# A four-branch decoder layer: when the projection's input is normalised, and where its gates are applied

## The chip, the cores and the metric

The kernel runs on one core of a Trainium2 chip. The metric is the device time of one execution in microseconds (us), as the median of several runs. The core's engines run side by side, each with a queue of its own that is worked off strictly in order: TensorE (matrix products; PE in the profile, its weight loads PEld), VectorE (DVE), ScalarE (ACT), GpSimd (POOL) and SyncE (SP, which here only issues DMA). An engine that meets a wait on a semaphore stands still with all that is queued behind it. TensorE reads only SBUF and writes PSUM; the PSUM has eight banks of 2 KB per partition.

## The reference, cut to what matters

Two layers of a hybrid decoder run over 256 prompt rows and 8 sample rows (264 columns in the kernel, which keeps features on the partitions). One layer:

```python
x = x + 0.5 * swiglu(rmsnorm(x, norm_ffn1), ...)
h = rmsnorm(x, norm_mix)                      # y = x * rsqrt(mean(x*x) + eps) * g
proj = h @ w_in                               # 3360 RWKV + 1536 short conv + 1544 Mamba columns
p_rwkv, p_sc, p_ssm = split(proj)
# RWKV group: token shift first
xs = p_rwkv + (prev - p_rwkv) * mu            # prev: the row before, or the state
r, k, v, w_lr, a_lr, g_lr = split(xs)         # then decay, keys' norm, LoRA gates, recurrence
# short convolution group
b_gate, c_gate, xt = split(p_sc, 3)
y_sc = rmsnorm(b_gate * causal_conv(c_gate * xt), sc_norm)
# Mamba group: convolution, silu, chunked scan (segments, scores), sample states
x = x + concat(y_rwkv, y_sc, y_ssm) @ w_out
x = x + 0.5 * swiglu(rmsnorm(x, norm_ffn2), ...)
```

## The kernel before, in words

Each layer has a front stage (first FFN, the projection, all that leads up to the recurrence) and a back stage (recurrence, output projection, second FFN). This case is about the second half of the front stage, the projection.

Weights are float32. A product is made in three fp32r products: weight and input are each split into a high part and a low rest. Per tile of 128 output columns TensorE multiplies 8 times (the 8 tiles of the 1024 features) by `hi*x_hi`, `hi*x_lo`, `lo*x_hi` (lines 232 to 234): 24 products of 264 columns. ScalarE makes `hi` of a weight tile (`split_hi`, line 209), VectorE or GpSimd makes `lo` (`split_lo`, line 216; GpSimd has the even tiles 14 to 24, and 44 and 46). Four such pairs are in a ring, so `split_hi(n + 4)` waits until product n is done.

The projection has 51 tiles, n = 0 to 50, each with a kind: n = 0 the tail (last RWKV columns and `dt`), 1 to 8 `xbc`, 9 and 10 RWKV tiles 24 and 25 (LoRA inputs), 11 to 14 `z`, 15 to 18 `x` of the short convolution, 19 to 22 its gate `c`, 23 to 26 its gate `b`, 27 to 34 the RWKV keys (8 to 15), 35 to 42 receptance (0 to 7), 43 to 50 values (16 to 23). The input of the products is `x * gain`, not yet divided by the root mean square; the factor `rs` (a row per column, the same on every partition) is multiplied in when VectorE evicts the tile from PSUM (`evict`, lines 1153 and 1159). Three PSUM banks take turns: product n + 3 waits for the eviction of tile n.

An RWKV tile is evicted to `prev`; ScalarE then writes `xs = (1 - mu) * prev` (line 1122) and keeps the last rows (`last`, line 1124); VectorE adds `mu` times the shifted columns (`shift`, line 1132). For a `c` tile VectorE multiplies a second time, into `u` (line 1162); for `b` all four tiles go to a buffer and one product over all four is made later (line 1290).

All other work of the front stage is woven into this sequence by hand. Every engine has a program `side`, a generator whose `yield s` says "what follows belongs to slot s"; `more.go(n)` in the loop over tiles runs what is due up to slot n. On VectorE, TensorE and GpSimd it stands after the work on tile n, on ScalarE before it. In each engine's queue the order is thus fixed. What matters here, by slot:

- TensorE: 12 transposes of `xa` into `b_tok`'s bank (line 1426), which wait for ScalarE's last SiLU (line 1004); 13, 15, 17, 19 a broadcast of two rows of `cum` (line 1443): the first waits for ScalarE's copy `b_tok` (line 1015), the others for VectorE's segments of the slot before; 16 to 22, even, products with the scores; 26 and 32 broadcasts of B and C rows for the sample states (line 1405), 26 also products with `xdt`; 35 mean of the short convolution's squares; 37 transposes of new states; 38 mean of the SSM squares (line 1507); 39 on LoRA products (line 1520 on), key norms and bonus products (line 1538).
- VectorE: 2 to 9 the Mamba convolution; 10 `cum_lo` and the sample convolution (lines 1212, 790 to 796); 11 `xdt`; 14, 16, 18, 20 segments (lines 1233, 1235, 1237); 15 to 21, odd, scores; 26 and 27 the four short convolutions; 28, 30, 33, 35 sample states (`sample`, `sample_out`); from 36 keys, gates and sums.
- ScalarE: 2 to 11 taps and SiLU; 13 `b_tok`; 15 on exponentials; 25 and 26 decay of the sample states (line 1047, 8 instructions per state tile); 27, 29, 32, 34 `outer` (line 1059), each after the first waiting for `sample_out` of the one before; 40 on the gates (lines 976 to 987), with a batch of Ln and Exp over the norms (lines 1091 to 1097) in slot 45, ahead of `gates(5)`.

## Time and profile before

| | |
|---|---|
| time, median of 3 runs | 1659.33 us (1658.1 to 1665.26) |
| profiled execution, its own time | 1660.52 us |
| its span in the profile | 1658.5 us |
| TensorE busy | 1550.0 us (93% of the span) |
| VectorE busy | 1145.6 us (69%) |
| ScalarE busy | 860.9 us (52%) |
| GpSimd busy | 264.0 us (16%) |
| mean granted TensorE clock | 0.986 |
| projection, layer 0 | 217.4 to 436.2 us |
| projection, layer 1 | 1033.0 to 1251.8 us |

The busy shares are averages over all stages. The time between the first product of the projection and the first of the back stage is what the change can touch. Matmuls are pipelined, so that a TensorE shown as busy can still have short gaps.

### The profile page before, as it was taken

How to read it: one execution, taken by the hardware profiler on the slowest of the kernel's cores; microseconds unless marked ns; L12 is line 12 of the kernel's file. 1: busy time of each engine (PE TensorE's matmuls, PEld its weight loads, DVE VectorE, ACT ScalarE, POOL GpSimd, SP SyncE). 2: the span in 40 equal slices, each digit the busy share in tenths (PEclk: the TensorE clock that was granted, in tenths of full speed). 3: DMA queues.
4: the chain of work that ended last, by engine and by line, in shares of the span. 5: the costliest groups of instructions: out<-in, count | busy, mean ns of one | idle time of the engine just before them, and what ended most of it. 6: DMA issues, size and time to landing. Idle time of an engine off the chain costs nothing. (4 is left out here: it accounts for less than half of the span.)

```text
span 1658.5 us, 41230 instructions
## 1 busy us (share of the span) xinstructions
PE 1550.0 (93%) x17275; PEld 1471.9 (89%) x17275; DVE 1145.6 (69%) x1832; ACT 860.9 (52%) x1521; POOL 264.0 (16%) x259
## 2 busy tenths in 40 slices
PE   7999999989799899999999999998997989899997
PEld 6999999977688789999999999998775878899997
DVE  6565578795798667665575656978768977676654
ACT  5444465767444555444354444657673445554443
POOL 0000003001455531000000000030014554300000
PEclk9999999999899999999999999999998999999999
DMA  7555557471244445555454655654703453465552
GB/s 232 178 168 176 161 157 211 131 210 52 64 127 119 138 150 171 196 174 187 149 186 153 203 166 175 194 157 131 213 1 104 126 166 111 130 199 181 187 176 71
DMA packets 280649, 256.26 MB, mean 155 GB/s; under 512 B 48054, under 2 KB 268700, under 8 KB 280450
## 3 DMA queue, kind: packets, MB, share of 16 engines
q1 hardware_dynamic: 276698, 252.05, 49.3%
q8 instruction: 138, 2.26, 0.6%
q10 hardware_dynamic: 3768, 1.59, 0.4%
q14 instruction: 45, 0.37, 0.1%
HBM read 242.22 MB, written 11.38 MB: 153 GB/s over the span
## 5 line engine op out<-in xcount | busy, mean ns | idle before, releaser
L209 ACT ACTIVATE front_hi<-front_raw 128x1024 fp32r<-128x1024 f32 (+2 forms) x230 | 238.5, 1039 | 257.2 <-PE ps L234 249.7
L216 DVE TENSOR_TENSOR front_lo<-front_raw,front_hi 128x1024 fp32r<-128x1024 f32 (+1 forms) x210 | 252.2, 1201 | 112.5 <-ACT front_hi L209 111.7
L209 ACT ACTIVATE out_hi<-out_raw 128x1024 fp32r<-128x1024 f32 (+1 forms) x168 | 173.2, 1038 | 216.1 <-PE ps L234 202.5
L216 DVE TENSOR_TENSOR out_lo<-out_raw,out_hi 128x1024 fp32r<-128x1024 f32 (+1 forms) x148 | 183.3, 1239 | 109.9 <-ACT out_hi L209 109.3
L232 PE MATMUL ps<-front_h_hi,front_hi 128*128 128x264 f32 (+1 forms) x816 | 241.2, 296 | 8.6 <-DVE front_lo L216 6.7
L234 PE MATMUL ps<-front_h_hi,front_lo 128*128 128x264 f32 (+1 forms) x816 | 233.0, 286 | 0.0
L233 PE MATMUL ps<-front_h_lo,front_hi 128*128 128x264 f32 (+1 forms) x816 | 232.8, 285 | 0.0
L232 PE MATMUL ps<-ffn_h_hi,out_hi 128*128 128x264 f32 x704 | 200.4, 285 | 0.1
L233 PE MATMUL ps<-ffn_h_lo,out_hi 128*128 128x264 f32 x704 | 199.6, 284 | 0.0
L234 PE MATMUL ps<-ffn_h_hi,out_lo 128*128 128x264 f32 x704 | 199.6, 283 | 0.0
L232 PE MATMUL ps<-in_h_hi,front_hi 128*128 128x264 f32 x688 | 197.3, 287 | 0.0
L233 PE MATMUL ps<-in_h_lo,front_hi 128*128 128x264 f32 x688 | 196.4, 285 | 0.0
L234 PE MATMUL ps<-in_h_hi,front_lo 128*128 128x264 f32 x688 | 196.3, 285 | 0.0
L232 PEld LDWEIGHTS ps<-front_h_hi,front_hi 128*128 128x128 f32 (+1 forms) x816 | 154.0, 189 | 16.8 <-issue 14.2
L233 PEld LDWEIGHTS ps<-front_h_lo,front_hi 128*128 128x128 f32 (+1 forms) x816 | 154.2, 189 | 0.7
L234 PEld LDWEIGHTS ps<-front_h_hi,front_lo 128*128 128x128 f32 (+1 forms) x816 | 153.5, 188 | 0.1
L216 POOL TENSOR_TENSOR front_lo<-front_raw,front_hi 128x1024 fp32r<-128x1024 f32 (+1 forms) x20 | 49.8, 2491 | 540.6 <-ACT front_hi L209 540.6
L232 PEld LDWEIGHTS ps<-ffn_h_hi,out_hi 128*128 128x128 f32 x704 | 132.4, 188 | 0.5 <-ACT ffn_h_hi L283 0.5
L233 PEld LDWEIGHTS ps<-ffn_h_lo,out_hi 128*128 128x128 f32 x704 | 132.4, 188 | 0.1
L234 PEld LDWEIGHTS ps<-ffn_h_hi,out_lo 128*128 128x128 f32 x704 | 132.4, 188 | 0.0
L233 PEld LDWEIGHTS ps<-in_h_lo,front_hi 128*128 128x128 f32 x688 | 131.2, 191 | 0.1
L232 PEld LDWEIGHTS ps<-in_h_hi,front_hi 128*128 128x128 f32 x688 | 131.1, 190 | 0.1
(410 smaller groups left out, 3861.2 us busy)
## 6 DMA issues: line engine op xcount, KB each, us to landing
front_raw<-in_w_in SPq DMA_DIRECT2D x50, 1024.0 KB, 5.4
out_raw<-in_ffn_w_in SPq DMA_DIRECT2D x44, 1024.0 KB, 5.2
front_raw<-in_ffn_w_in SPq DMA_DIRECT2D x40, 1024.0 KB, 5.3
back_sample_rows<-row_scratch SPq DMA_DIRECT2D x160, 128.0 KB, 3.1
out_raw<-in_w_out SPq DMA_DIRECT2D x16, 1024.0 KB, 5.8
front_raw<-in_ffn_w_out SPq DMA_DIRECT2D x16, 896.0 KB, 5.0
out_raw<-in_ffn_w_out SPq DMA_DIRECT2D x16, 896.0 KB, 4.9
front_raw<-in_ffn_w_out SPq DMA_DIRECT2D x8, 1024.0 KB, 5.4
```

What stands on the lines that cost most here:

```text
L209: act.activation(self.hi[n % self.RING][:, 0:k, 0:w], self._raw(n), ACT.Copy).then_inc(self.hi_ready, 1)
L216: eng.tensor_tensor(self.lo[n % self.RING][:, 0:k, 0:w], self._raw(n), self.hi[n % self.RING][:, 0:k, 0:w].bitcast(F32), ALU.subtract).the ...
L232: pe.matmul(out, hi[:, j, 0:w], x_hi[:, j], start=start and j == 0, stop=False)
L233: pe.matmul(out, hi[:, j, 0:w], x_lo[:, j], start=False, stop=False)
L234: mm = pe.matmul(out, lo[:, j, 0:w], x_hi[:, j], start=False, stop=stop and j == k - 1)
```

## The change

Tiles 0 to 18 are computed as before, from `x * gain` (now held in `env.in_hi` and `env.in_lo`). Meanwhile VectorE and ScalarE make a second input, `x * gain * rs`, split in `h_hi` and `h_lo`: per feature tile k one step `normed(k)` and one `normed_lo(k)` on VectorE and one `normed_hi(k)` on ScalarE, in slots 10 to 18. From tile 19 on (`NORMED = 19`; the twentieth tile) the products use that, so that what stands in PSUM is final: a `c` tile is multiplied onto `u` straight from PSUM, a `b` tile onto the convolution's result, and an RWKV tile goes without `prev`: ScalarE writes `xs` and `last` from PSUM, then VectorE adds the shifted columns from PSUM (`mix_shifted`) and frees the bank. The `b` tiles move from 23 to 26 to 31 to 34, behind the keys, which are now 23 to 30; two of the four short convolutions move from slots 26 and 27 to 31 and 32, the squares of the short convolution to slot 35 of ScalarE with a buffer of their own, its mean to slot 36 of TensorE. ScalarE's batch of Ln and Exp is cut in two halves, slots 46 and 47, behind `gates(5)`.

```diff
-("c", SC0 + 512, 0, 4), ("b", SC0, 0, 4), ("rwkv", 8 * P, 8, 8), ("rwkv", 0, 0, 8),
+("c", SC0 + 512, 0, 4), ("rwkv", 8 * P, 8, 8), ("b", SC0, 0, 4), ("rwkv", 0, 0, 8),
-        H = len(tiles)
+        H, NORMED = len(tiles), 19
-        z, bg = at("z", 20832, [P, 4, N]), at("b_gate", 25056, [P, 4, N])
+        z, sc_squares = at("z", 20832, [P, 4, N]), at("sc_squares", 25056, [P, 4, N])
-        norm2 = Norm(st, env, "mix", lambda k: env.col("norm_mix", k), A, h_hi, h_lo, rs, xa, ctmp[:, 0])
+        norm2 = Norm(st, env, "mix", lambda k: env.col("norm_mix", k), A, env.in_hi, env.in_lo, rs, xa, ctmp[:, 0])
...
 # GpSimd, slot 42
                     pool.wait_ge(s("state_out"), 64)
+                    pool.wait_ge(s("sc_ms"), 1)
...
 # ScalarE
+                def normed_hi(k):
+                    act.wait_ge(s("normed"), k + 1)
+                    act.activation(h_hi[:, k], ctmp[:, k % 2], ACT.Copy).then_inc(s("normed_hi"), 1)
...
                         yield slot
+                        if slot == 11:
+                            normed_hi(0)
                         if slot < 10:
...
+                    yield 12
+                    normed_hi(1)
                     yield 13
+                    normed_hi(2)
                     act.wait_ge(s("btok_ps"), 1)
                     act.activation(btok[:].rearrange("p c g n -> p (c g n)"), ps[:, A, :], ACT.Copy).then_inc(s("btok_done"), 1)
                     yield 14
+                    normed_hi(3)
...
                         yield 15 + h // 2 * 2
+                        if h in (0, 2):
+                            normed_hi(4 + h)
+                            normed_hi(5 + h)
...
-                        if m == 3:
-                            act.wait_ge(s("sc_gated"), 1)
-                            act.wait_ge(s("bc_ps"), 2)
-                            act.activation(sq, acc, ACT.Square).then_inc(s("sc_sq"), 1)
...
+                    yield 35
+                    act.wait_ge(evicted, 35)
+                    act.activation(sc_squares[:], acc, ACT.Square).then_inc(s("sc_sq"), 1)
                     yield 37
                     act.wait_ge(s("y_gated"), 1)
-                    act.wait_ge(s("sc_ms"), 1)
+                    act.wait_ge(s("bc_ps"), 2)
...
                     for p, slot in enumerate((40, 41, 42, 43, 44, 45, 48, 49)):
-                        yield slot
-                        if p == 5:
+                        if p == 6:
+                            yield 46
                             act.wait_ge(s("norm_max"), RT)
...
+                            yield 47
                             act.wait_ge(s("norm_ln"), 3)
...
+                        yield slot
                         gates(p)
...
 # ScalarE, loop over the tiles
                     more.go(n)
+                    if kind == "rwkv" and n >= NORMED:
+                        act.wait_ge(ws.used, base + n + 1)
+                        bank = ps[:, n % 3, 0:N]
+                        act.activation(mix.xs[:, m], bank, ACT.Copy, scale=env.omu[:, m:m + 1]).then_inc(kept, 1)
+                        act.activation(last[:, m], bank[:, T - 1:T + NS], ACT.Copy).then_inc(last_in, 1)
                     ws.split_hi(act, base + n + 4)
-                    if kind in ("rwkv", "tail"):
+                    if kind in ("rwkv", "tail") and n < NORMED:
...
 # VectorE
+                    if kind == "c":
+                        dve.wait_ge(evicted, n)
+                        dve.tensor_tensor(u[:, m, 2:2 + N], u[:, m, 2:2 + N], bank, ALU.mult).then_inc(evicted, 1)
+                        return
+                    if kind == "b":
+                        dve.wait_ge(s("smp_sc"), 5)
+                        dve.wait_ge(s("uconv"), 3 * (m + 1))
+                        dve.tensor_tensor(acc[:, m], acc[:, m], bank, ALU.mult).then_inc(evicted, 1)
+                        return
...
+                def mix_shifted(n, m):
+                    q, bank = order.index(m), ps[:, n % 3, 0:N]
+                    dve.wait_ge(kept, q + 1)
+                    dve.wait_ge(last_in, q + 1)
+                    dve.scalar_tensor_tensor(out=mix.xs[:, m, 1:T], in0=bank[:, 0:T - 1], scalar=env.col("rwkv_mu", m),
+                                             in1=mix.xs[:, m, 1:T], op0=ALU.mult, op1=ALU.add).then_inc(evicted, 1)
+
+                def normed(k):
+                    if k >= 2:
+                        dve.wait_ge(s("normed_lo"), k - 1)
+                    dve.scalar_tensor_tensor(out=ctmp[:, k % 2], in0=env.x[:, k], scalar=env.col("norm_mix", k), in1=rs[:],
+                                             op0=ALU.mult, op1=ALU.mult).then_inc(s("normed"), 1)
+
+                def normed_lo(k):
+                    dve.wait_ge(s("normed_hi"), k + 1)
+                    dve.tensor_tensor(h_lo[:, k], ctmp[:, k % 2], h_hi[:, k].bitcast(F32), ALU.subtract).then_inc(s("normed_lo"), 1)
...
                     yield 10
+                    normed(0)
                     dve.wait_ge(s("cum_hi"), 1)
...
                     yield 11
+                    normed(1)
                     dve.wait_ge(s("tok_in"), 1)
...
+                    yield 12
+                    normed_lo(0)
+                    normed(2)
+                    yield 13
+                    normed_lo(1)
+                    normed(3)
                     for j in range(4):
                         yield 14 + 2 * j
+                        if j < 2:
+                            for t in (2 + 2 * j, 3 + 2 * j):
+                                normed_lo(t)
+                                normed(t + 2)
+                        if j == 2:
+                            normed_lo(6)
+                            normed_lo(7)
                         for h in (2 * j, 2 * j + 1):
...
 # VectorE, slots 26 to 36: short_conv(0) in 26, (1) in 27, sample(0) 28, conv_sample 29, sample(1) 30,
 # short_conv(2) 31, short_conv(3) and the new states 32, sample(2) 33, sample(3) 35, sc_root and y_gated 36
...
 # VectorE, loop over the tiles
+                    late = kind == "rwkv" and n >= NORMED
-                    if n < H:
+                    if n < H and not late:
                         evict(n, kind, m)
...
                     if n + 3 < H and ws.on_dve[base + n + 3]:
                         ws.split_lo(dve, base + n + 3)
+                    if late:
+                        mix_shifted(n, m)
                     more.go(n)
...
 # TensorE
-                    yield 35
+                    yield 36
                     pe.wait_ge(s("sc_sq"), 1)
...
+                def normed_ready(j):
+                    pe.wait_ge(s("normed_lo"), j + 1)
...
+                    hi, lo = (env.in_hi, env.in_lo) if n < NORMED else (h_hi, h_lo)
+                    ws.product(pe, base + n, ps[0:halves[base + n][2], n % 3, 0:N], hi, lo,
+                               ready={0: norm2.pe_ready(pe), NORMED: normed_ready}.get(n))
```

## Rows read from the trace of the kernel before

**Rows 1.** Stretches: start:end, length, busy of each engine (instructions), granted clock, DMA share, GB/s.
```profile
261.00:303.00 42.00, 41.33 (x332) 37.91 (x332) 30.91 (x72) 22.84 (x32) 13.21 (x5) 1.00 0.53 164
303.00:369.00 66.00, 58.75 (x454) 56.71 (x450) 58.54 (x101) 45.60 (x113) 0.16 (x1) 0.97 0.60 174
...
1033.00:1251.80 218.80, 198.46 (x1469) 179.62 (x1467) 172.14 (x323) 142.19 (x278) 28.20 (x22) 0.98 0.45 133
```

**Rows 2.** TensorE by line, 217.4 to 436.2: busy us, mean ns, idle before and releasers.
```profile
L232 PE MATMUL ps<-front_h_hi,front_hi 128*128 128x264 f32 x400 | 118.3, 296 | 3.7 <-DVE front_lo L216 3.4 <-DVE z L1159 0.2
...
L1520 PE MATMUL ps<-xs,w_a 64*128 64x264 f32 x16 | 5.7, 435 | 1.3 <-ACT conv_new_rows L1078 0.8 <-ACT gate L987 0.5
...
L1538 PE MATMUL ps<-r_k,cst 128*128 128x264 f32 x16 | 5.1, 444 | 4.3 <-DVE r_k L1334 4.3
...
L1405 PE MATMUL ps<-bc_rows,pick_row 16*128 16x256 f32 x16 | 2.3, 284 | 2.5 <-DVE outer L1173 2.5
...
L1507 PE MATMUL ps<-xbc_conv,cst 128*128 128x264 f32 x8 | 2.0, 399 | 1.2 <-ACT xbc_conv L1070 1.2
```

**Rows 3.** A stretch of layer 0 with a low granted clock, columns as in rows 1.
```profile
339.20:342.40 3.20, 3.20 (x17) 3.20 (x16) 3.20 (x11) 3.20 (x11) 0.00 (x0) 0.50 0.12 14
```

**Rows 4.** VectorE by line and shape, 217.4 to 436.2, columns as in rows 2.
```profile
L216 DVE TENSOR_TENSOR front_lo<-front_raw,front_hi 128x1024 fp32r<-128x1024 f32 x40 | 48.6, 1215 | 1.8 <-ACT front_hi L209 1.8
...
L1153 DVE TENSOR_TENSOR front_prev<-ps,front_norm_rs 128x264 f32<-128x264 f32 x26 | 11.1, 428 | 18.4 <-PE ps L234 18.4
...
L1334 DVE SCALAR_TENSOR_TENSOR r_k<-xs,cols 128x264 f32<-128x264 f32 x8 | 3.6, 483 | 0.0
...
L1162 DVE TENSOR_TENSOR gated<-gated,c_gate 128x264 f32<-128x264 f32 x4 | 1.7, 433 | 0.1
```

**Rows 5.** ScalarE in order of time: start us, us, instruction [idle before, releaser].
```profile
260.82 0.49 ACT L1004 ACTIVATE xbc_conv<-xbc_conv,cols 128x256 f32<-128x256 f32 x1
...
263.59 0.58 ACT L1015 ACTIVATE b_tok<-ps 128x512 f32<-128x512 f32 x1
...
308.24 4.78 ACT L1047 ACTIVATE sample_state<-sample_state,spread 128x128 f32<-128x128 f32 x16
...
401.32 1.28 ACT L1091 ACT_TABLE_LOAD   x1
...
409.66 1.28 ACT L976 ACT_TABLE_LOAD   x1
```

**Rows 6.** VectorE in order of time, projection and start of the back stage.
```profile
261.82 0.41 DVE L1212 TENSOR_TENSOR cum_rows<-cum,cum_rows 8x256 fp32r<-8x256 f32 x1
...
263.87 2.35 DVE L796 TENSOR_TENSOR xbc_conv<-xbc_conv,outer 128x64 f32<-128x64 f32 x1
...
266.40 0.42 DVE L1159 TENSOR_TENSOR z<-ps,front_norm_rs 128x264 f32<-128x264 f32 x1
...
273.09 0.14 DVE L1237 COPY cum_last<-ps 128x1 f32<-128x1 f32 x1
...
279.76 0.14 DVE L1237 COPY cum_last<-ps 128x1 f32<-128x1 f32 x1
...
442.96 1.74 DVE L2133 SCALAR_TENSOR_TENSOR bonus<-bonus,cols,gate 128x264 f32<-128x264 f32 x2
```

**Rows 7.** TensorE in order of time: the broadcasts of slots 13, 15 and 17.
```profile
266.17 0.50 PE L1443 MATMUL ps<-cum_rows,pick_row_far 40*128 40x256 f32 x2
...
273.31 0.47 PE L1443 MATMUL ps<-cum_rows,pick_row_far 40*128 40x256 f32 x2
...
280.74 0.50 PE L1443 MATMUL ps<-cum_rows,pick_row_far 40*128 40x256 f32 x2
```

**Rows 8.** GpSimd in order of time: two weight splits, one step of the back stage.
```profile
263.76 2.38 POOL L216 TENSOR_TENSOR front_lo<-front_raw,front_hi 128x1024 fp32r<-128x1024 f32 x1 [4.13 <-ACT front_hi L209]
...
278.11 2.63 POOL L216 TENSOR_TENSOR front_lo<-front_raw,front_hi 128x1024 fp32r<-128x1024 f32 x1 [4.05 <-ACT front_hi L209]
...
443.54 0.87 POOL L1750 TENSOR_TENSOR back_a_r<-kk_normed,back_decays 128x256 f32<-128x256 f32 x1
```

More of the change, by code:

```diff
@@ L1264, in side @@
                                           ALU.mult).then_inc(s("xde_done"), 1)
-                    done = 0
-                    for i in range(4):
-                        yield 26 + i // 2
-                        if i == 0:
-                            dve.wait_ge(s("xa_smp"), 1)
-                            dve.wait_ge(s("spread_in"), 1)
-                            dve.tensor_tensor(xs_dt[:], xa[:, 0:4, T:N], spread[:, :, NS:2 * NS], ALU.mult).then_inc(s("xs_dt"), 1)
-                        dve.wait_ge(s("u_done"), ST)
-                        done = conv_prompt(dve, s("uconv"), acc[:, i, 0:T], u[:, i], lambda j: env.col("sc_conv_w", 4 * j + i), 3, done)
@@ new lines, in side @@
+                    yield 27
+                    short_conv(1)
+                    yield 28
+                    sample(0)
+                    sample_out(0)
+                    yield 29
+                    scb = env.scb[:].rearrange("p m (b j) -> p m b j", j=2)
+                    conv_sample(dve, s("smp_sc"), acc[:, :, T:N], scn[:, :, 0:NS], [scb[:, :, :, 0], scb[:, :, :, 1], u[:, :, 2 + T:2 + N]],
+                                lambda j: env.col("sc_conv_w", 4 * j, 4))
+                    yield 30
@@ new lines, in side @@
+                    sample(1)
+                    sample_out(1)
+                    yield 31
+                    short_conv(2)
+                    yield 32
+                    short_conv(3)
+                    dve.wait_ge(s("smp_sc"), 5)
+                    cvb = env.conv[:].rearrange("p m (b j) -> p m b j", j=3)
+                    scw = scn[:, :, 2:18].rearrange("p m (b j) -> p m b j", j=2)
+                    cvw = cvn[:, :, 3:27].rearrange("p m (b j) -> p m b j", j=3)
+                    dve.tensor_copy(scn[:, :, 0:2], u[:, :, T:T + 2]).then_inc(s("new_in"), 1)
@@ L1301, in side @@
+                    yield 33
+                    sample(2)
+                    sample_out(2)
+                    yield 35
+                    sample(3)
+                    sample_out(3)
+                    yield 36
+                    dve.wait_ge(s("sc_ms"), 1)
+                    dve.tensor_scalar(sc_root[:], ps[:, EB, 0:N], D / SC, NORM_EPS, ALU.mult, ALU.add).then_inc(s("sc_read"), 1)
                     dve.wait_ge(s("smp"), 4)
@@ L1390, in _ @@
                         before = tiles[n - 1][1]
-                        shift(before)
+                        if n - 1 < NORMED:
+                            shift(before)
                         if before in (25, 15, 7):
```

64 lines of the change are left out of this document (23 added, 41 removed).

## Prediction, made before the changed kernel ran

> **What bounds it now.** I read the stretch table first [rows 1]. In the projection (217.4 to 436.2 us in layer 0; layer 1's stretch is the same 218.8 us) TensorE is busy for all but 0.7 of 42 us between 261 and 303, and for all but 7.3 of 66 between 303 and 369, where VectorE is busy for 58.5. So matrix work bounds the first part, and VectorE and TensorE together the second. The lines of TensorE [rows 2] say how much idle time can be won back: the products wait 3.4 us for weight splits (half at tile 3, before the change begins, so 1.7 at tile 32), the second row broadcast waits 2.5 for `outer`, the SSM mean 1.2, the LoRA products 0.8 and 0.5; the bonus products' 4.3 lie mostly behind the last tile, where the order stays. So 6.7 us in the middle of a layer could go with lighter VectorE work, and some clock with them: from 339.2 to 342.4, right behind the waits of 1.7 and 2.5, the granted clock is 0.50 (1.2 instead of 2.4 GHz) [rows 3]; 3.2 us at half speed lose 1.6.
>
> **What the edit removes and adds** [rows 4]. From tile 23 on, 24 evictions of 0.43 us go (pitch in the queue 0.35): 8.4 us a layer; the mixing step stays at its price but now reads PSUM. The `c` tiles lose four multiplies of 0.43; the `b` tiles lose one over all four tiles, as large as a weight split (1.2). Against it stand 8 three-operand steps (the nearest row of that shape is 0.48) and 8 subtractions (0.43): 16 instructions, 6.2 us of VectorE at their pitches of 0.40 and 0.35. ScalarE gets 8 copies, about 0.5 each (its SiLU over a tile, 0.49, is the nearest row [rows 5]). So VectorE's sum falls by some 5 us. It is the place that matters: what is taken away lies behind tile 19, what is added lies in slots 10 to 18, where TensorE is the bound and VectorE is already late.
>
> **Slots 10 to 13.** VectorE begins slot 10 at 261.8 and evicts tile 11 only at 266.4 [rows 6], when TensorE, at 266.2, is already past product 13 [rows 7]. New in its queue first is `normed(0)`, done at 262.2. ScalarE's slot 11 starts with `normed_hi(0)`, which waits for it; behind it in the queue stands the last SiLU, now at 260.82 [rows 5], which TensorE's transposes of slot 12 await. It becomes 262.7: TensorE 1.9 us late. Next, VectorE: slot 10 without the stall told below ends near 264.6, eviction, shift, `normed(1)` at 265.8, two `xdt` products to 267.0, eviction of tile 12, a weight split to 268.5. Then `normed_lo(0)`, then `normed(2)`. ScalarE's slot 13 is `normed_hi(2)` ahead of the copy into `b_tok`, now at 263.59, and TensorE's row broadcast of slot 13 (now at 266.17) waits for that copy.
> How late `normed(2)` is depends on GpSimd. Its weight split of tile 16 runs 263.76 to 266.14, and a VectorE sum of 64 columns with both inputs in SBUF takes 2.35 in it, a sixteenth of a split's work [rows 6, 8]. In the back stage, at 443, two-input steps of VectorE take 0.87 each (1.74 for two) instead of 0.48 beside GpSimd operations of 0.87: each waits for the other in turn, so the one that is waiting comes next. Steps that read PSUM pass unhindered: the segment steps and copies up to 279.9 lie inside GpSimd's 278.11 to 280.74. In the new order GpSimd's split of tile 16 (released by ScalarE near 267.5) waits for VectorE's split to 268.5, holds it to 270.9, and both new operations come after: `normed(2)` at 271.8, `normed_hi(2)` 272.3, `b_tok` 272.9. The broadcast moves from 266.2 to 272.9: 6.7 us, less 0.2 that tile 14 waits for an eviction today [rows 2] = **6.5**.
> The Trainium skill ("SBUF — State Buffer", section "Who interferes with whom") says the same: a VectorE instruction with two SBUF inputs and a GpSimd one that reads SBUF exclude each other for a whole instruction. By it too the change is slower; without the lock the sum would be rival 2's.
>
> **Slots 14, 16, 18.** The new four, four and two operations stand ahead of the segment steps, directly behind a VectorE weight split, just when GpSimd's split of tiles 18, 20, 22 (about 2.4 us alone) is waiting: today that of tile 20 starts at 278.11 in the midst of VectorE's and the segments follow. Slot 14: 1.6 of work of its own + 2.4 = 4.0, cover 0.2 (segments end at 273.23, the broadcast starts at 273.31): **3.8**. Slot 16: 4.0 less a cover of 0.8 (279.9 to 280.74): **3.2**. Slot 18: 0.75 + 2.4 less about 0.9: **2.2**, partly as product 19 waiting for `normed_lo(7)`. Without the port the three are 1.4, 0.8 and 0.
> Clock: waits of some 5, 4 and 3 us are each longer than those that went before the fall at 339.2. One such spell, 1.6 us; bounds 0 and three. I take **1.6**.
>
> **Tiles 19 to 50.** Late tiles free their PSUM bank through ScalarE first (`kept`, then `last`), then VectorE. ScalarE decays sample states in slot 25 (16 instructions, 4.8 us [rows 5]) ahead of tile 25's copy. VectorE's `mix_shifted(25)` waits for that, and behind it stands `xdt`, for which slot 26 of TensorE waits. Tile 24 done = 0: tile 25's copy at about 7.5 (two earlier copies and a weight split, 0.6 of small reads, 4.8), `xdt` 9.2; TensorE wants it at 7.1. **+2.1**; bounds 0 and 3.
> At tiles 30 to 32 two convolutions fewer precede `sample(1)`, but tile 29's copy waits behind `outer(1)`, itself behind `sample_out(0)`: today's 1.7 + 2.5 + 1.6 stay. Value 0, bounds -5.8 and +1.
> Slots 35 to 40: squares of the short convolution now need tile 34's gate, behind `sample(2)`; TensorE's slot 36 could wait 4.0. Against it, the SSM mean and the first LoRA products no longer wait (1.2, 0.8, 0.5). Between +1.5 and -2.5 I take the middle, **-0.5**.
> Slots 45 to 49: the Ln and Exp batch (8.3 us from its first table load to the next) moves behind `gates(5)`. Slot 48 of TensorE needs `gates(6)`, behind the second half: up to 2 late by my count, while slot 46's bonus products may lose up to 1 of their wait. Between -1 and +2: **+0.5**. SP and the DMA queues keep their slots; state stores 3 and 4 move with slot 35, and the first gates, some 15 us behind it, still find them done: nothing.
>
> **Sum.** 6.5 + 3.8 + 3.2 + 2.2 + 1.6 + 2.1 + 0 - 0.5 + 0.5 = 19.4 us a layer, 38.8 for two. The profiled execution took 1660.52 for a span of 1658.5; the median is 1659.33. 1659.3 + 38.8 = **1698 us**.
>
> **Rivals.** 1: as summed, 1698. Chance 0.50.
> 2: the chain bites but GpSimd's splits fall elsewhere: 1.9 + 2.5 + 1.4 + 0.8 - 0.2 + 2.1 = 8.5 a layer: 1676. For it: ScalarE's lateness shifts the splits. Against: GpSimd's release comes one ScalarE split after the product, every time. Chance 0.15.
> 3: more: three clock spells (+3.2), slot 36 and slot 48 in full (+3.5): 26.1 a layer, 1711. Chance 0.17.
> 4, the other side: the lighter VectorE wins. If VectorE's lateness at slot 12 is made up so that the chain of slots 10 to 18 is hidden, the waits at tiles 32 to 39 (1.7 + 2.5 + 1.2 + 0.8 + 0.5) and the clock spell (1.6) vanish: -8.3 a layer, 1643. It decides once slots 10 to 18 cost under 8 us a layer. For it: VectorE is busy for only 30.9 of the 42 us from 261 to 303 [rows 1]. Against: each broadcast reads what VectorE made one tile earlier, with covers of 0.2 and 0.8 us. Chance 0.10.
> 5: the loss and these gains cancel, 1659. Chance 0.08.
>
> **Numbers.** 0.5% (8 us) is about what a measurement of this kernel can tell from no change. Slower = 1 + 2 + 3 = 0.82, same 0.08, faster 0.10. The range takes in rival 2 with some of the later gains (1664) and rival 3 (1712); it leaves out rivals 4 and 5. The likeliest case alone: 1690 to 1706.
>
> **What would show it.** Right: ScalarE's copy of `b_tok` some 9 us later; VectorE's first `normed_lo` and those of slots 14 to 18 at 2 us and more, inside GpSimd's splits; TensorE waiting 3 to 5 us in slots 13, 15 and 17 (for ScalarE's copy, then VectorE's segments); a granted clock of 0.5 after them; tile 19 starting some 14 us later. Wrong: new operations at 0.4 to 0.5 us with TensorE dense up to tile 19; then the projection is shorter through tiles 29 to 39, and rival 4 holds.

## The result, and the profile after

The changed kernel takes **1722.3 us** (median; 1717.3 to 1724.1) against 1661.5 for the kernel before on the same chip: ratio 1.036, 95% interval 1.033 to 1.039. It is slower, as forecast, and by the chain that was forecast, but by 61 us instead of 38.8, which lies outside the range (1664 to 1712). A layer is 30.6 us longer: the back stage of layer 0 starts at 466.77 instead of 436.17.

The stretch table of the changed kernel comes first, cut so that each stretch holds the same matmuls as one of before (332 in 261 to 303 [rows 1], then 815 in 303 to 436.2):

```profile
261.00:326.40 65.40, 51.57 (x332) 47.52 (x332) 42.63 (x83) 25.61 (x40) 14.18 (x5) 0.82 0.34 105
326.40:466.80 140.40, 122.41 (x815) 108.26 (x812) 91.22 (x161) 87.97 (x202) 8.38 (x12) 0.92 0.34 102
```

The same table of the kernel before, for the second stretch:

```profile
303.00:436.20 133.20, 116.30 (x815) 102.58 (x812) 101.38 (x187) 89.62 (x202) 10.40 (x12) 0.97 0.36 108
```

Two numbers are to be read in each row: TensorE's busy time, and what is left of the length. In the first stretch the idle time rises from 0.7 to 13.8 us (+13.2), and the *same 332 matmuls* take 51.6 instead of 41.3 us (+10.2), with a granted clock of 0.82 instead of 1.00. In the second, idle time rises by 1.1 and the same 815 matmuls take 6.1 us more. So a layer's 30.6 us are 14.3 us of waiting and 16.3 us of clock. The prediction had 17.8 and 1.6.

TensorE in order of time (start, us, instruction, idle before and what ended it), to be laid beside [rows 7]:

```profile
272.32 0.50 PE L1513 MATMUL ps<-cum_rows,pick_row_far 40*128 40x256 f32 x2 [2.85 <-ACT b_tok L1025]
...
284.49 0.77 PE L1513 MATMUL ps<-cum_rows,pick_row_far 40*128 40x256 f32 x2 [4.13 <-DVE cum_last L1294]
...
285.80 0.42 PE L234 MATMUL ps<-in_h_hi,front_lo 128*128 128x264 f32 x1
...
291.79 0.28 PE L234 MATMUL ps<-in_h_hi,front_lo 128*128 128x264 f32 x1
...
297.78 0.77 PE L1513 MATMUL ps<-cum_rows,pick_row_far 40*128 40x256 f32 x2 [3.14 <-DVE cum_last L1294]
```

The broadcasts wait 2.85, 4.13 and 3.14 us (2.84, 4.13 and 3.16 in layer 1). Behind them a matmul of a product takes 0.42 us instead of 0.28, with starts 0.22 apart instead of 0.12: from 297.8 to 304.1 the granted clock is 0.50 (1.2 GHz). Product 16 needs 5.5 us and product 18 5.7, instead of 3.2 (of product 14 only a part is slow: 14 and 15 together take 7.6 instead of 6.4). Product 17, between them, has full speed again, and the next wait takes it away. One wait stands ahead of these three: 2.17 us ahead of the transposes of slot 12, with the clock at 0.50 behind it too. Product 19 of the changed kernel starts at 304.9 instead of 285.1, 19.8 us later.

VectorE in order of time:

```profile
268.39 0.43 DVE L1204 TENSOR_TENSOR front_h_lo<-c_gate,front_h_hi 128x264 fp32r<-128x264 f32 x1
268.86 2.47 DVE L1199 SCALAR_TENSOR_TENSOR c_gate<-x,cols,front_norm_rs 128x264 f32<-128x264 f32 x1
...
278.99 2.59 DVE L1204 TENSOR_TENSOR front_h_lo<-c_gate,front_h_hi 128x264 fp32r<-128x264 f32 x1
...
282.90 0.48 DVE L1290 SCALAR_TENSOR_TENSOR segments<-ps,tok_cum_dt,cst 128x256 f32<-128x256 f32 x1
...
292.23 2.63 DVE L1204 TENSOR_TENSOR front_h_lo<-c_gate,front_h_hi 128x264 fp32r<-128x264 f32 x1
```

GpSimd and ScalarE in order of time:

```profile
267.29 3.74 POOL L216 TENSOR_TENSOR front_lo<-front_raw,front_hi 128x1024 fp32r<-128x1024 f32 x1 [7.83 <-ACT front_hi L209]
278.70 2.58 POOL L216 TENSOR_TENSOR front_lo<-front_raw,front_hi 128x1024 fp32r<-128x1024 f32 x1 [7.67 <-ACT front_hi L209]
```

```profile
271.36 0.42 ACT L992 ACTIVATE front_h_hi<-c_gate 128x264 fp32r<-128x264 f32 x1 [4.14 <-DVE c_gate L1199]
271.69 0.58 ACT L1025 ACTIVATE b_tok<-ps 128x512 f32<-128x512 f32 x1
```

Read together: in slot 12 VectorE's `normed(2)` takes 2.47 us beside GpSimd's split (267.29 to 271.03) and ends at 271.33, ScalarE's `normed_hi(2)` stands waiting for it, and the copy into `b_tok` behind that comes at 271.69 instead of 263.59. In slots 14 and 16 the first subtraction takes 2.6 us for 0.43 us of work, beside a GpSimd split of 2.6, and the segments, for which TensorE waits, start behind it.

### The profile page after: what moved, and what is told of

Same layout as the page of the kernel before. It is cut to its first block and busy times, and to the rows that moved or that the text cites. A ratio compares the mean times of both kernels' runs of the same rounds, so it can differ in the third digit from the quotient of the medians.

```text
span 1719.7 us, 41234 instructions
## 1 busy us (share of the span) xinstructions
PE 1583.2 (92%) x17275; PEld 1503.5 (87%) x17275; DVE 1149.0 (67%) x1806; ACT 862.3 (50%) x1537; POOL 261.0 (15%) x259
## 5 line engine op out<-in xcount | busy, mean ns | idle before, releaser
L232 PE MATMUL ps<-in_h_hi,front_hi 128*128 128x264 f32 x992 | 290.4, 293 | 4.8 <-DVE front_lo L216 3.3
L233 PE MATMUL ps<-in_h_lo,front_hi 128*128 128x264 f32 x992 | 286.8, 289 | 0.0
L234 PE MATMUL ps<-in_h_hi,front_lo 128*128 128x264 f32 x992 | 286.6, 289 | 0.0
L233 PEld LDWEIGHTS ps<-in_h_lo,front_hi 128*128 128x128 f32 x992 | 192.0, 194 | 0.2
L234 PEld LDWEIGHTS ps<-in_h_hi,front_lo 128*128 128x128 f32 x992 | 190.8, 192 | 0.1
L232 PE MATMUL ps<-front_h_hi,front_hi 128*128 128x264 f32 x512 | 157.8, 308 | 2.1 <-DVE front_h_lo L1204 2.0
L233 PE MATMUL ps<-front_h_lo,front_hi 128*128 128x264 f32 x512 | 151.1, 295 | 0.0
L234 PE MATMUL ps<-front_h_hi,front_lo 128*128 128x264 f32 x512 | 151.0, 295 | 0.0
L232 PEld LDWEIGHTS ps<-front_h_hi,front_hi 128*128 128x128 f32 x512 | 102.8, 201 | 7.8 <-issue 3.8
L233 PEld LDWEIGHTS ps<-front_h_lo,front_hi 128*128 128x128 f32 x512 | 102.7, 201 | 0.6
```

Source lines behind the costliest of these rows:

```text
L232: pe.matmul(out, hi[:, j, 0:w], x_hi[:, j], start=start and j == 0, stop=False)
L233: pe.matmul(out, hi[:, j, 0:w], x_lo[:, j], start=False, stop=False)
L234: mm = pe.matmul(out, lo[:, j, 0:w], x_hi[:, j], start=False, stop=stop and j == k - 1)
```

## The experiments

All times are medians; each ratio is to the kernel before, run on the same chip with it, whose time stands in the third column. It differs by up to 3.4 us from row to row, so a difference between rows with different times there is that uncertain; the text gives plain differences of medians. Lines named are those of the kernel that ran; `...` marks lines of code left out. Stretches and waits are those of layer 0.

| run | us | before, us | ratio, 95% interval |
|---|---|---|---|
| changed kernel | 1722.3 | 1661.5 | 1.036 (1.033 to 1.039) |
| e1 ScalarE's order | 1709.4 | 1658.9 | 1.030 (1.028 to 1.033) |
| e2 segments first | 1688.7 | 1658.9 | 1.018 (1.016 to 1.020) |
| e3 both orders | 1683.9 | 1658.9 | 1.015 (1.013 to 1.016) |
| e4 splits on VectorE | 1694.6 | 1658.9 | 1.022 (1.020 to 1.023) |
| e5 before, 2 additions | 1696.6 | 1660.2 | 1.022 (1.019 to 1.025) |
| e6 before, 4 additions | 1707.9 | 1660.2 | 1.029 (1.027 to 1.031) |
| e7 e3, decays behind | 1686.2 | 1660.2 | 1.016 (1.014 to 1.017) |
| e8 e3, batch in slot 45 | 1693.2 | 1660.2 | 1.020 (1.017 to 1.023) |
| e9 e3, three more orders | 1680.5 | 1660.5 | 1.013 (1.011 to 1.015) |
| e10 e9, splits on VectorE | 1676.1 | 1660.5 | 1.010 (1.008 to 1.012) |
| e11 no background work | 1671.5 | 1660.5 | 1.007 (1.006 to 1.009) |
| e12 e11, two orders | 1674.5 | 1660.5 | 1.008 (1.007 to 1.010) |
| e13 waits filled | 1706.1 | 1658.1 | 1.029 (1.027 to 1.030) |
| e14 copies ahead | 1662.6 | 1658.1 | 1.0024 (1.0015 to 1.0034) |
| e15 e14, tail earlier | 1661.7 | 1659.0 | 1.0018 (1.0006 to 1.0031) |

### Where the waits come from: e1 to e4

**e1**, on the changed kernel:

```diff
-                        if slot == 11:
-                            normed_hi(0)
                         if slot < 10:
...
                                            bias=env.col("ssm_conv_b", i)).then_inc(s("xa_done"), 1)
+                        if slot == 11:
+                            normed_hi(0)
...
-                    normed_hi(2)
                     act.wait_ge(s("btok_ps"), 1)
...
+                    normed_hi(2)
```

> Edit: on ScalarE alone, the hi copy of input tile 0 goes behind the last SiLU and that of tile 2 behind the b_tok copy; nothing else differs from the changed kernel. Theory (each wait of TensorE costs itself and half clock behind it): the waits of 2.17 us ahead of L1496 and 2.85 us ahead of the broadcast of slot 13 go, and with them some 2.5 us per layer of products 13 to 15 at half clock: about 7 us per layer, 1722 becomes about 1708. Rival (VectorE's queue is what is late, ScalarE's order only shows it): the wait moves to the broadcast of slot 15, which grows from 4.13 us to 6 or more, and the time falls by 4 us at most.

1709.4: 13 us faster (10 against the kernel before of each), near the theory's number, but not quite by its waits. The wait ahead of the transposes fell to 0.45 and that of slot 13 to 1.67 (from 2.85); the one of slot 15 grew from 4.13 to 5.22. One us of the rival is in it.

**e2**, on the changed kernel: the same background work, behind the segments on VectorE (shown) and behind the second exponential on ScalarE.

```diff
                         yield 14 + 2 * j
-                        if j < 2:
-                            for t in (2 + 2 * j, 3 + 2 * j):
-                                normed_lo(t)
-                                normed(t + 2)
-                        if j == 2:
-                            normed_lo(6)
-                            normed_lo(7)
                         for h in (2 * j, 2 * j + 1):
...
+                        if j < 2:
+                            for t in (2 + 2 * j, 3 + 2 * j):
+                                normed_lo(t)
+                                normed(t + 2)
+                        if j == 2:
+                            normed_lo(6)
+                            normed_lo(7)
```

> Edit: in slots 14, 16 and 18 VectorE's segments go ahead of the normed ops, and ScalarE's exponentials ahead of its hi copies of slots 15 and 17; the rest is the changed kernel. Theory: the waits of 4.13, 3.14 and 0.81 us ahead of the broadcasts of slots 15, 17 and 19 go, and the half clock of products 16, 18 and 20 (2.3, 2.4 and 1.5 us): about 14 us per layer, 1722 becomes about 1694. Rival (the work on VectorE and ScalarE is simply too much for these slots): evictions and scores are late instead, TensorE waits for them, and the gain is under 8 us.

1688.7: 34 us. The waits of slots 15, 17 and 19 are 0.22, 0 and 0; those of slots 12 and 13 stay.

**e3**: both edits.

> Edit: both reorderings together, on the changed kernel. Theory: the two gains add, about 21 us per layer, 1722 becomes about 1680, and the granted clock of slots 10 to 18 is 0.95 or more. Rival (too much work there in any order): at least 1710, with the same number of waits over 2 us of TensorE, at other instructions.

1683.9: 38 us, of 42 expected. The stretch with the same 332 matmuls:

```profile
261.00:307.60 46.60, 41.78 (x332) 38.23 (x332) 39.09 (x83) 25.53 (x40) 13.97 (x5) 1.00 0.49 149
```

The idle time is 4.8 us (13.8 in the changed kernel) and the matmuls are back to 41.8 us: 9.0 us of waiting took 9.8 us of clock with them. Here waits of 1.69 and 1.33 us stand ahead of products that take 3.2 us.

**e4**, on the changed kernel:

```diff
-                                                                    *range(base + 48, base + H, 2)})
+                                                                    *range(base + 14, base + 26, 2), *range(base + 48, base + H, 2)})
```

> Edit: the weight splits of tiles 14 to 24 that GpSimd makes go to VectorE (1.2 us each there), so that no GpSimd operation of 2.6 us stands beside a normed op; all orders as in the changed kernel. Theory (the normed_lo ops are held by GpSimd's split, 2.6 us instead of 0.43): each of slots 14, 16 and 18 gets 2.2 us shorter and VectorE 1.2 us of split longer somewhere in the two slots: the waits of slots 15 and 17 fall to 2 to 3 and 1 to 2 us, 3 to 4 us per layer with the clock behind them, about 1715. Rival (VectorE's load decides, not the hold): 6 splits of 1.2 us more on VectorE make it 4 to 10 us slower, 1726 to 1732.

1694.6: 28 us faster with *six operations of 1.2 us more* on VectorE. The hold by GpSimd's split is a cause by itself, and the expectation under-rated it fourfold: the waits of slots 15, 17 and 19 fell to 1.96, 0.96 and 0, and products 18 and 20 ran at 3.2 us each. Only slot 13's grew (3.67). One gain was not forecast: the wait of slot 12 went as well. GpSimd's split of tile 14 had held VectorE's convolution steps ahead of `normed(0)` (three of them took 3.71 us, here 1.52), so that here `normed(0)` starts at 259.91 instead of 261.53.

### What a wait costs: e5, e6, e13

**e5** and **e6** put nothing of the change into the kernel before, only VectorE work ahead of its segments (e6 has 4 where e5 has 2):

```diff
                         yield 14 + 2 * j
+                        for i in range(2 if j < 3 else 0):
+                            if 2 * j + i:
+                                dve.wait_ge(s("gap"), 2 * j + i)
+                            dve.tensor_tensor(outer[:, 1:7].rearrange("p b n -> p (b n)"), env.x[:, 0:3].rearrange("p k n -> p (k n)")[:, 0:768],
+                                              env.x[:, 1:4].rearrange("p k n -> p (k n)")[:, 0:768], ALU.add).then_inc(s("gap"), 1)
                         for h in (2 * j, 2 * j + 1):
```

> Edit: the kernel before, with two chained VectorE additions of 128x768 into unused space ahead of the segments of slots 14, 16 and 18; nothing of the change is in it. It prices a wait of TensorE by itself. By the row of L216 (1.22 us for 1024 columns) the two take about 1.9 us. Theory (a wait costs itself, and half clock only where it is long): TensorE waits 1 to 2 us in each of slots 15, 17 and 19, the granted clock stays at 1.00, and the kernel is 3 x 1.5 = 4.5 us per layer longer, about 1668. Rival (any wait ahead of these broadcasts brings half clock): 8 us per layer, about 1675.

1696.6, 28 us above the 1668 that was expected. It was no test of short waits: two additions took 4.1 us, not 1.9, since in the kernel before too a GpSimd split stands there and holds them. TensorE waited 4.07, 3.25 and 3.25 us, and products 16, 18 and 20 took 4.7, 5.4 and 5.6 us instead of 3.2. So 10.6 us of waits brought 6.2 us of clock.

> Edit: as the run with two additions, with four (about 3.8 us) in each of the three slots. Theory (clock as the missing term): TensorE waits about 3.5 us ahead of each of three broadcasts as in the changed kernel, products 16, 18 and 20 take 4.7 to 5.6 us instead of 3.2, and a layer gets 10.5 us of waits and some 6 us of clock longer: about 1659 + 33 = 1692. Rival (the clock falls for another reason that is in the change and not here, such as fewer matmuls in the slots or the normed ops themselves): the waits alone, about 1659 + 21 = 1680, with the products at 3.2 us.

1707.9, above both expectations (the four additions took 5.96 us). TensorE's broadcasts by line:

```profile
L1447 PE MATMUL ps<-cum_rows,pick_row_far 40*128 40x256 f32 x8 | 2.7, 436 | 16.4 <-DVE cum_last L1241 16.4
```

Waits of 5.92, 5.23 and 5.23 us, products of 4.9, 4.5 and 5.6: 5.5 us of clock. Against e5 the waits grew by 5.8 us a layer and the clock by nothing. At these lengths the clock costs about 2 us per wait, not per microsecond waited. So the changed kernel's own work is not needed for slow matmuls: the kernel before shows them with nothing but VectorE's additions and the waits.

**e13** leaves the changed kernel's delays and takes the standing still away:

```diff
                         yield 13 + 2 * j
+                        if j < 3:
+                            pe.wait_ge(evicted, 12 + 2 * j)
+                            for i in range(24):
+                                pe.matmul(ps[:, (14 + 2 * j) % 3, 0:N], env.in_hi[:, i % 8, 0:P], env.in_hi[:, 7 - i % 8],
+                                          start=True, stop=True)
```

> Edit: the changed kernel, with 24 extra matmuls of 264 columns (a product's number, 3.2 us at full clock) into the accumulator of the next tile ahead of each of the waits of slots 13, 15 and 17; the next product writes over them. Theory (half clock follows from TensorE standing still): the waits of 2.85, 4.13 and 3.14 us shrink to about 0, 1 and 0 us, products 14, 16 and 18 take 3.2 us instead of up to 5.6, and the kernel gets some 5 us per layer faster with 72 matmuls more in each layer: about 1712. Rival (the clock falls for another reason, or with the load): the products keep their 5.5 us, the fillers run at half clock too, and the time is 1722 or more.

1706.1: 16 us faster (13 against the kernel before of each) with 144 matmuls more. TensorE in order of time, slots 15 and 17, and its stretch from 261:

```profile
282.48 0.47 PE L1517 MATMUL ps<-cum_rows,pick_row_far 40*128 40x256 f32 x2 [1.18 <-DVE cum_last L1294]
...
283.35 0.28 PE L232 MATMUL ps<-in_h_hi,front_hi 128*128 128x264 f32 x1
...
293.13 0.47 PE L1517 MATMUL ps<-cum_rows,pick_row_far 40*128 40x256 f32 x2 [0.18 <-DVE cum_last L1294]
```

```profile
261.00:319.00 58.00, 53.48 (x404) 49.75 (x404) 42.15 (x83) 25.63 (x40) 14.25 (x5) 0.94 0.36 114
```

The matmuls behind the filled waits take 0.28 us. Products 14, 16 and 18 take 3.0 to 3.2; product 20, whose wait was not filled, still 4.7. The fillers take nothing off VectorE's work: they only kept TensorE going. So it is TensorE's standing still that brings the half clock. The wait of slot 12, which was not filled, still has half clock behind it.

### The later tiles: e7 to e12, e14, e15

**e7**, on e3: ScalarE's 64 decays of slots 25 and 26 go behind the copies of these tiles.

```diff
                 for n, (kind, m) in enumerate(tiles):
-                    more.go(n)
+                    if n not in (25, 26):
+                        more.go(n)
                     if kind == "rwkv" and n >= NORMED:
...
                         act.activation(last[:, m], bank[:, T - 1:T + NS], ACT.Copy).then_inc(last_in, 1)
+                    more.go(n)
```

> Edit: on the kernel with both reorderings (1683.9), ScalarE's work of slots 25 and 26 (the 64 decays of the sample state) goes behind the two copies of these tiles instead of ahead. Theory (VectorE's late tile waits for ScalarE's copy behind 16 decays, and the xdt product behind it): xdt is ready before TensorE asks, its wait of 2.10 us and about 1.4 us of half clock go: 3.5 us per layer, about 1677. Rival (the decays are then late for the state sums of slot 28, and the wait ahead of the second broadcast grows from 1.89 us by the same): within 2 us of 1684.

1686.2: the rival. The `xdt` wait went, but product 30 waited 2.31 us and product 32 waited 3.75 us for VectorE's late-tile operation, which had been 1.05.

**e8**, on e3: ScalarE's logarithms (Ln) and exponentials (Exp) in one batch ahead of `gates(5)`, as before the change.

```diff
-                        if p == 6:
-                            yield 46
+                        if p == 5:
+                            yield 45
...
-                            yield 47
                             act.wait_ge(s("norm_ln"), 3)
```

> Edit: on the kernel with both reorderings (1683.9), ScalarE's logarithms and exponentials go back together ahead of the gates of slot 45, as in the kernel before. Theory: the wait of 2.60 us ahead of L1590 in slot 48 and the half clock of the product behind it (2.2 us, and 0.8 in the small matmuls) go, and a wait of 1.3 us ahead of L1608 in slot 46 comes, as in the kernel before: 4 us per layer, about 1676. Rival (the end of the stage hangs on VectorE's r_k, 3.24 us, which absorbs it): within 2 us of 1684.

1693.2: wrong in sign, 9 us slower. ScalarE, VectorE and TensorE in order of time (the batch's first table load starts at 411.87):

```profile
419.20 0.47 ACT L1137 ACTIVATE xs<-ps,one_minus_mu 128x264 f32<-128x264 f32 x1
```

```profile
419.84 0.48 DVE L1192 SCALAR_TENSOR_TENSOR xs<-ps,cols,xs 128x255 f32<-128x255 f32 x1 [10.33 <-ACT last_rows L1138]
```

```profile
422.39 2.13 PE L1607 MATMUL ps<-r_k,cst 128*128 128x264 f32 x4 [7.37 <-DVE r_k L1399]
```

A late tile's VectorE operation first waits for ScalarE's two copies of the same tile, and these stand behind whatever ScalarE's slot holds: 10.3 us here. The old form's eviction waited for TensorE alone. In one piece the batch makes TensorE wait 7.4 us, more than it does cut in two.

**e9** adds to e3: `xdt` ahead of tile 25, the squares ahead of the last state products, the gates of pair 6 in slots 45 and 46. **e10** adds e4's splits.

```diff
-                    yield 25
                     dve.wait_ge(s("dend_exp"), 1)
...
                         yield 27 + 2 * m + m // 2
+                        if m == 3:
+                            act.wait_ge(evicted, 35)
+                            act.activation(sc_squares[:], acc, ACT.Square).then_inc(s("sc_sq"), 1)
...
-                    for p, slot in enumerate((40, 41, 42, 43, 44, 45, 48, 49)):
-                        if p == 6:
+                    for p, slot in enumerate((40, 41, 42, 43, 44, 45, 46, 49)):
+                        if p == 7:
...
-                        if slot < 45 or 47 <= slot < 49:
-                            p = slot - 39 if slot < 45 else slot - 41
+                        if slot < 46 or slot == 48:
+                            p = slot - 39 if slot < 46 else 7
```

> Edit: the kernel with both reorderings (1683.9) and three more: VectorE's xdt product ahead of tile 25 instead of behind it, ScalarE's squares of the short convolution ahead of the last state row products, and the gates of head pair 6 one to two slots earlier, ahead of the logarithms. Theory (each long wait costs itself and about 2 us of half clock): the waits of 2.10 us ahead of L1554 (and 1.4 us of clock), 2.96 us ahead of L1561 (1.7) and 2.60 us ahead of L1590 in slot 48 (3.0) go: 13.8 us per layer, about 1656, level with the kernel before. Rival (VectorE and ScalarE are filled in these stretches, and what is put ahead makes the next thing late): at least 1675.

> Edit: the run before this one, and the GpSimd splits of tiles 14 to 24 on VectorE. In the changed kernel that move alone gave 28 us, through waits that the reorderings have since removed. Theory (the hold by GpSimd's split is what is left behind the waits of 1.69, 1.33 and 0.99 us in slots 13, 15 and 19): 2 us per layer less than the run before. Rival (nothing is held any more, and VectorE's six splits of 1.2 us count): 1 to 3 us per layer more than the run before.

1680.5 and 1676.1. e9 is mostly the rival's: the wait ahead of the mean fell from 2.96 to 1.05, and the next one, for `sc_root`, went from 0.34 to 5.64; the wait for `xdt` went, and product 32's grew from 1.05 to 3.79. e10's 4 us are the theory's. What stays in e10 is seen in ScalarE, VectorE and TensorE in order of time:

```profile
333.42 2.18 ACT L1072 ACTIVATE outer<-ps,sample_xdt 128x128 f32<-128x128 f32 x8 [4.90 <-DVE y_short L1219]
```

```profile
336.13 0.48 DVE L1193 SCALAR_TENSOR_TENSOR xs<-ps,cols,xs 128x255 f32<-128x255 f32 x1 [1.44 <-ACT last_rows L1139]
```

```profile
336.67 0.59 PE L232 MATMUL ps<-front_h_hi,front_hi 128*128 128x264 f32 x1 [3.78 <-DVE xs L1193]
```

ScalarE waits 4.9 us for VectorE's state sum, tile 29's copies wait behind it, VectorE waits for them, and TensorE for the bank.

**e11** takes the background work and the late form out (all tiles read the unnormalised input, each eviction multiplies) and keeps the moves; **e12** adds two of e9's orders (squares, gates).

```diff
-        H, NORMED = len(tiles), 19
+        H, NORMED = len(tiles), 99
...
                         dve.wait_ge(evicted, n)
-                        dve.tensor_tensor(u[:, m, 2:2 + N], u[:, m, 2:2 + N], bank, ALU.mult).then_inc(evicted, 1)
+                        dve.tensor_tensor(ctmp[:, m % 2], bank, rs[:], ALU.mult).then_inc(s("gate_in_sb"), 1)
+                        dve.wait_ge(s("gate_in_sb"), m + 1)
+                        dve.tensor_tensor(u[:, m, 2:2 + N], u[:, m, 2:2 + N], ctmp[:, m % 2], ALU.mult).then_inc(evicted, 1)
...
-                        dve.tensor_tensor(acc[:, m], acc[:, m], bank, ALU.mult).then_inc(evicted, 1)
+                        dve.wait_ge(evicted, n)
+                        dve.tensor_tensor(sc_squares[:, m], bank, rs[:], ALU.mult).then_inc(s("gate_in_sb"), 1)
+                        dve.wait_ge(s("gate_in_sb"), m + 5)
+                        dve.tensor_tensor(acc[:, m], acc[:, m], sc_squares[:, m], ALU.mult).then_inc(evicted, 1)
...
-                    hi, lo = (env.in_hi, env.in_lo) if n < NORMED else (h_hi, h_lo)
+                    hi, lo = h_hi, h_lo
...
```

> Edit: the changed kernel without its background normalisation: all tiles take the unnormalised input and are multiplied by the reciprocal root at eviction as before, the gates with two operations; the second gates stand behind the keys, and the later work is ordered as in the changed kernel. Theory (the loss is the background work of slots 10 to 19, and the split of the logarithm batch costs at slot 48): slots 10 to 33 take the time of the kernel before, slots 33 to 47 1 to 2 us less, slot 48 5 us more: 1659 + 2 x 3.5, about 1666. Rival (the late tiles gained something that the order alone does not): about 1675 or more. Rival (the split of the batch costs only because the late tiles' VectorE operations wait for ScalarE's copy): about 1657.

> Edit: the run before this one, with ScalarE's squares ahead of the last state row products and the gates of head pair 6 ahead of the logarithms. Theory: the waits ahead of the mean of slot 36 and of the gates of slot 48 go with their clock, 5 to 8 us per layer: about 1652, faster than the kernel before. Rival (the stage's end hangs on VectorE, 3 us ahead of L1608, which takes up what is won): within 3 us of the run before.

1671.5 and 1674.5. So of the 61 us the moves cost about 11, and the background work with the late tiles, by the difference, about 50. In e11 product 27 starts at 315.40 (315.27 before): nothing is lost up to there. Then product 32 waits 2.70 us (1.74 before) for a weight split, and 3.04 us come ahead of the mean of slot 36, with half clock behind it, and 1.98 ahead of slot 48's gates; the back stage starts 6.0 us later. So the moves alone, without the late form, already spoil these places. e12 shows e9's move again: 5.60 us for `sc_root`.

**e14**, on e10, with the squares back in slot 35:

```diff
                 for n, (kind, m) in enumerate(tiles):
-                    more.go(n)
+                    if not 27 <= n < 36:
+                        more.go(n)
                     if kind == "rwkv" and n >= NORMED:
...
                         act.activation(last[:, m], bank[:, T - 1:T + NS], ACT.Copy).then_inc(last_in, 1)
+                    more.go(n)
```

> Edit: the kernel with all orders and the splits on VectorE (1676.1), with ScalarE's two copies of the late tiles ahead of its other work in slots 27 to 35, and the squares back in slot 35. Theory (VectorE's operation of a late tile waits for ScalarE's copy, which stands behind ScalarE's wait for VectorE's state sums): the wait of 3.78 us ahead of product 32 and the half clock behind it (2.5 us) go, and the wait ahead of the transposes of slot 37 (5.64 us) is back to 0.3 with 3 us ahead of the mean: 6 to 8 us per layer, about 1662. Rival (VectorE has too much to do in slots 28 to 36): the wait stays over 2 us, at the same place or at the row broadcast of slot 32, and the time is within 4 us of 1676.

1662.6, as expected: 13.5 us (11 against the kernel before of each) from the order of two copies against the rest of ScalarE's slot and the squares put back, which were not tried apart. A wait of 2.31 us stayed at product 32. **e15** moves the end of the stage forward.

```diff
-                        for p in {44: (0, 1), 46: (2, 3), 49: (4, 5), 50: (6, 7)}.get(slot, ()):
+                        for p in {44: (0, 1), 46: (2, 3), 48: (4, 5), 50: (6, 7)}.get(slot, ()):
...
-                        if slot in (47, 49, 50):
-                            cumulate({47: 5, 49: 6, 50: 7}[slot])
-                        if slot in (43, 45, 48, 50):
-                            for p in {43: (0, 1), 45: (2, 3), 48: (4, 5), 50: (6, 7)}[slot]:
+                        if slot in (46, 47, 49):
+                            cumulate({46: 5, 47: 6, 49: 7}[slot])
+                        if slot in (43, 45, 47, 49):
+                            for p in {43: (0, 1), 45: (2, 3), 47: (4, 5), 49: (6, 7)}[slot]:
...
```

> Edit: the kernel of the run before (1662.6), with the end of the stage one slot earlier: gates of head pair 7 in slot 48, VectorE's cumulative sums of pairs 5 to 7 in slots 46, 47 and 49, its r_k products of pairs 4 to 7 in slots 47 and 49, the bonus products of pairs 4 and 5 in slot 49, and TensorE's matmuls for them in slot 48. Theory (VectorE stands idle 3.2 and 3.5 us in slots 46 to 48 and is full from slot 49 on, and the end waits for it): the wait of 4.09 us shrinks by 2 to 3 us and half clock behind it with it, 2.5 us per layer: about 1657.5, just faster than the kernel before. Rival (the next stage waits for VectorE's whole remaining work, which starts no earlier): within 1.5 us of 1662.6.

1661.7: the rival, within 1 us. The last wait fell from 4.09 to 0.34, another of 2.27 came two products earlier, and the next stage waited 4.41 us instead of 2.95. e14 and e15 are 0.2% slower than the kernel before, with intervals that lie just above 1: about level, not faster.

## Why the prediction was wrong

**The step that failed** is the clock term: "waits of some 5, 4 and 3 us are each longer than those that went before the fall at 339.2. One such spell, 1.6 us; bounds 0 and three. I take **1.6**." The condition was right and the count was not. A layer loses 16.3 us more to the clock than before, 10.2 in slots 10 to 26 and 6.1 later: seven spells more than before, at 1.2 to 3.0 us each (the wait's own length not counted). They stand behind the waits of 2.17, 2.85, 4.13, 3.14, 2.10 and 2.61 us, and behind two short ones close together (0.98 and 0.81, products 19 and 20). The 1.89 of slot 32 has one too, as the kernel before has there; there is none behind the 2.88 of slot 36 and the 1.98 that follows. Taken alone, the row of the one spell did not say whether the price comes once or with each wait; even rival 3, with three spells, had 4.8. But the trace of the kernel before did: its other wait of over 2 us in the projection, 3.01 us ahead of the last bonus products (427.74 to 430.74), also has half clock behind it, and so in layer 1.

```profile
431.20:441.40 10.20, 6.47 (x52) 4.15 (x51) 4.80 (x8) 2.41 (x6) 0.96 (x5) 0.50 0.06 9
```

e5, e6 and e13 show the cause. The Trainium skill ("TensorE: Matmul & The Clock Gate", section "HAM oscillation — how this bites in real kernels") describes a kernel that pays for a cold clock after each pause again; the traces agree for most of the long waits, with some 2 us at each. The waits came out 3.5 us a layer below the forecast (14.3 instead of 17.8), which hid a part of the miss.

**Slots 10 to 13** (6.5): right in place and in lateness. The broadcast of slot 13 starts 6.15 us later. But only 5.0 us of it are waits (2.17 and 2.85, where 0.4 and nearly 0 stood before); most of the rest is half clock behind the first of them. GpSimd's split met `normed(2)` rather than `normed_lo(0)`, which still slipped through at 0.43; the end was forecast for 271.8 and is 271.3. The Trainium skill's exclusion of two-input VectorE and GpSimd operations ("SBUF — State Buffer", section "Who interferes with whom") holds here: 2.5 and 2.6 us for operations of 0.48 and 0.43.

**Slots 14, 16, 18** (3.8, 3.2, 2.2): waits of 4.13, 3.14, and 0.98 + 0.81. Right, each within some 0.4. Idle time in slots 10 to 26 grew by 13.2; these terms and the 6.5 make 15.7.

**Tile 25 and `xdt`** (2.1): 2.10 on the row, and some 2.7 us of clock behind it (the 16 products with `xdt` take 3.8 us instead of 2.05, the next ones are slow too).

**Tiles 30 to 32** (0): one wait of 1.89 in place of 1.74 and 2.47, so -2.3, inside the bounds. **Slots 35 to 40** (-0.5): 2.88 and 1.98 in place of 1.64, 1.23, 0.80 and 0.48, so +0.7. **Slots 45 to 49** (+0.5): slot 48 waits 2.61 and slot 46 0.9 less, so +1.7, and 3 us of clock follow.

**Rival 4** asked for under 8 us in slots 10 to 18. e10 shows it tried: there slots 10 to 26 cost 2 us, and the kernel was still 15.6 us slower. Its gains at tiles 32 to 39 did not come. The late tiles bring a new dependence on ScalarE's queue (e8, e10, e14), which the prediction saw at tile 25 and at tile 29 only; and the moves alone cost there too (e11).

Left open: what exactly remains between e14 and a gain. VectorE is busy for 92.0 us of the last 132.9 in e14 (101.4 of 133.2 before), so the relief is there, and none of it reached the end. Waits were not laid out one by one by length, and at some 2 to 3 us the runs show both: half clock behind 1.96 (e4), 2.10, 2.17 and 2.61 us, none behind 1.98 and 2.88. What decides there is not known. Nor was the move of GpSimd's splits to VectorE (e4) tried on the kernel before, so how much of its gain needs the change is open.

## What to carry to other kernels

Where TensorE is dense, cost a new wait of 3 us at its length and about 2 us of half clock, each time, not once; a reordering that removes it gives both back (e2, e3). Work that is "in the background" is so only if it stands behind what the busiest engine waits for in each queue, and beside no GpSimd operation that reads SBUF if it has two SBUF inputs. Before an eviction is made to follow another engine's copy, look at what else stands in that engine's slot.

## What the runs showed of the hardware that was not expected

- 144 useless matmuls made the kernel 16 us faster (e13).
- Waits of 3.25 and 5.23 us cost the same clock: products 18 and 20 took 5.4 and 5.6 us behind the one, 4.5 and 5.6 behind the other (e5, e6; 3.2 at full speed).
- Two VectorE additions of 128x768 took 4.1 us and four 6.0 beside one GpSimd split: the hold of some 2 us comes once, not with each addition.
- Six weight splits moved from GpSimd (2.6 us each) to VectorE (1.2 each), which was the engine in question, made the kernel 28 us faster (e4).
